# More places in the weight ring until the first projection ends: six, then five, then four again

## What is computed

```
mod = SiLU(cond) @ w_mod[l] + b_mod[l]            # 1024 x 6144, for two vectors cond
h   = RMSNorm(x) * (1 + scale1) + shift1
qkv = h @ w_in[l]                                 # three head groups: A, B and C
x   = x + gate1 * (attention(qkv) @ w_out[l])
h2  = RMSNorm(x) * (1 + scale2) + shift2
x   = x + gate2 * PEER(h2)                        # top 16 of 128^2 experts, 8 heads
```

## Time and profile before

| | us |
|---|---|
| median of 3 runs | 4315.52 (4315.12, 4315.52, 4328.44) |
| the profiled execution, own time | 4312.1 |
| its span | 4310.0 |
| PE busy in the span | 2889.9 |
| DVE busy | 2803.9 |
| ACT busy | 1465.4 |
| POOL busy | 1282.5 |
| mean granted TensorE clock | 0.818 of full |

### The profile page before, as it was taken

The page is one execution under the profiler, slowest core; times in us unless marked ns, Lnnn a source line. Parts: engine busy times, 40 slices in busy tenths (PEclk is TensorE's granted clock), DMA queues, the critical chain, the costliest instruction groups (busy, mean ns, idle before and its releaser), DMA issues.

```text
span 4310.0 us, 47615 instructions
## 1 busy us (share of the span) xinstructions
PE 2889.9 (67%) x16592; PEld 1297.9 (30%) x16592; DVE 2803.9 (65%) x5874; ACT 1465.4 (34%) x4706; POOL 1282.5 (30%) x1306
## 2 busy tenths in 40 slices
PE   6887788766666566665656978886555565555665
PEld 4555565332221122221112566542111111111111
DVE  1167887697646755665675789669764674674554
ACT  2113675322223322222233468533222222222222
POOL 1002222123333333333333222112333333343332
PEclk9898899887887777777877989998777768777767
DMA  8447897669999999999998778666999999999997
GB/s 292 176 154 293 346 361 262 229 248 396 402 414 405 402 411 402 411 408 417 416 408 340 266 252 292 223 228 243 406 419 421 417 415 417 414 416 418 415 421 326
DMA packets 230192, 1508.71 MB, mean 350 GB/s; under 512 B 25408, under 2 KB 29504, under 8 KB 64960
## 3 DMA queue, kind: packets, MB, share of 16 engines
q0 software_dynamic: 185504, 1353.53, 78.4%
q1 hardware_dynamic: 44448, 152.14, 9.6%
HBM read 1501.38 MB, written 4.19 MB: 349 GB/s over the span
## 4 chain that ended last, share of the span: by engine, by line
DMA 41%; PE 26%; DVE 20%; issue 6%; ACT 5%; POOL 2%; SPq 0%; ACTq 0%; DVEq 0%; POOLq 0%
DMA work<-expert_dram,work 39%; PE psum L893 10%; DVE work L1792 5%; PE psum L925 4%; DVE work L1836 3%; PE psum L738 3%; PE psum L831 3%; DVE work L1844 2%; POOL work L2054 2%; ACT work L1266 1%; PE psum L808 1%; DMA ring<-w_mod_dram 1%; PE psum L742 1%; PE psum L792 1%; DVE stat L1580 1%
## 5 line engine op out<-in xcount | busy, mean ns | idle before, releaser
L893 PE MATMUL psum<-work 64*64 64x512 f32 x8192 | 1428.2, 827 | 1103.1 <-ACT work L1266 1103.1
L1792 DVE SCALAR_TENSOR_TENSOR work<-work,psum 128x1024 f32<-128x1024 f32 x1024 | 1247.6, 1220 | 991.2 <-DMA work<-expert_dram,work 987.2
L2054 POOL DMA_INDIRECT work<-expert_dram,work x1024 | 978.4, 955 | 1739.6 <-PE psum L893 1608.1
L893 PEld LDWEIGHTS psum<-work 64*64 64x64 f32 x8192 | 328.8, 168 | 2144.3 <-ACT work L1266 1877.9
L1257 ACT ACTIVATE work<-work 128x2 f32<-128x2 f32 x512 | 104.1, 203 | 1913.4 <-DVE work L1792 1913.3
L2036 POOL DMA_INDIRECT work<-expert_dram,work x256 | 274.7, 1073 | 1180.2 <-DVE work L1836 874.4
L1844 DVE SCALAR_TENSOR_TENSOR work<-work 128x1024 f32<-128x1024 f32 x256 | 313.2, 1224 | 106.0 <-DMA work<-expert_dram,work 105.5
L1266 ACT ACTIVATE work<-const,work 128x128 f32<-128x128 f32 x1024 | 347.4, 386 | 0.0
L1836 DVE SCALAR_TENSOR_TENSOR work<-work 128x1024 f32<-128x1024 f32 x254 | 326.9, 1287 | 15.2 <-ACT work L1297 14.7
L845 PE MATMUL psum<-work,ring 128*128 128x512 f32 x512 | 231.5, 607 | 30.5 <-ACT work L1110 30.5
L1260 ACT ACTIVATE work<-work 128x1 f32<-128x1 f32 x1024 | 245.7, 287 | 16.8
(11 more groups left out here) (199 smaller groups left out, 2887.6 us busy)
## 6 DMA issues: line engine op xcount, KB each, us to landing
ring<-w_mod_dram SPq DMA_DIRECT2D x96, 512.0 KB, 6.1
ring<-w_in_dram SPq DMA_DIRECT2D x80, 512.0 KB, 4.6
ring<-w_query_dram SPq DMA_DIRECT2D x64, 512.0 KB, 6.0
work<-expert_dram,work POOLq DMA_INDIRECT x1280, 8.8
ring<-w_out_dram SPq DMA_DIRECT2D x32, 512.0 KB, 6.5
work<-rpb_dram POOLq DMA_DIRECT2D x2, 2688.0 KB, 17.0
xT<-xT_dram SPq DMA_DIRECT2D x1, 2560.0 KB, 11.8
work<-tables_dram POOLq DMA_DIRECT2D x2, 1024.0 KB, 9.5
```

The source lines that it names most:

```text
L893: last = pe.matmul(out[to:to + HP, cols_], diag[tok, n % NDIAG, tok], rows[(SLOTS * t + s) % NBUF][tok, D + 512 * half:D + 512 * half + 51 ...
L1792: dve.scalar_tensor_tensor(u, u, 1.0, pair[0], ALU.mult, ALU.mult, accum_out=act_in[:, s:s + 1]).then_inc(dot_done, 1)
L2054: pool.indirect_dma_start(rows[m % NBUF], None, a[f"expert{l}"], bass.IndirectOffsetOnAxis(expert[:, t % 2, s:s + 1], 0)).then_inc(row_in[ ...
```

## The change

Two places are added to the ring, in pieces of `work` that are idle for the time: place 4 at `H_AT + KC * NLAT`, place 5 (`SUM_PLACE`) on `csum`. Both serve up to block `win 0 12`; up to `win 0 19` place 4 does; from then on the four of `ring` alone. A block no longer goes to place n % 4 but to the allowed place that was, by a table made at build time, released first: `last[p]` is the number of the block that stood there, and for a `win` of the first layer that number plus `INNER[i]`, the count of blocks that PE takes before it is done with it. The order of the loads, the order of PE's work and all sizes stay. DVE gets one wait more, for all uses of place 5 to be over, ahead of the first write to `csum`.

```diff
+MORE = 2
+SUM_PLACE = RING + 1
+SUM_BLOCK = 13
...
+    place, count, uses, last = [], [], [0] * (RING + MORE), [-1] * (RING + MORE)
+    for n, (what, l, i) in enumerate(ORDER):
+        allowed = RING
+        if n < BLOCK["win", 0, SUM_BLOCK]:
+            allowed = RING + 2
+        elif n <= BLOCK["win", 0, NWIN - 1]:
+            allowed = RING + 1
+        p = min(range(allowed), key=lambda x: last[x])
+        place.append(p)
+        count.append(uses[p])
+        uses[p] += 1
+        last[p] = n + INNER[i] + 0.5 if what == "win" and l == 0 else n
...
+        ring_more = [at(H_AT + KC * NLAT, KC, P), at(X_AT + D, KC, P)]
...
-                if n >= RING:
-                    sp.wait_ge(freed[n % RING], n // RING)
-                sp.dma_start(ring[:, n % RING], weights[what][l, i]).then_inc(landed[n % RING], 16)
+                if COUNT[n]:
+                    sp.wait_ge(freed[PLACE[n]], COUNT[n])
+                sp.dma_start(ring_at(n), weights[what][l, i]).then_inc(landed[PLACE[n]], 16)
...
-                pe.wait_ge(landed[n % RING], 16 * (n // RING + 1))
-                return ring[:, n % RING]
+                pe.wait_ge(landed[PLACE[n]], 16 * (COUNT[n] + 1))
+                return ring_at(n)
...
                     dve.wait_ge(ctx_coef, SLOTS * l + s + 1)
+                    if l == 0 and s == 0:
+                        dve.wait_ge(freed[SUM_PLACE], PLACE.count(SUM_PLACE))
```

More of the change, by code:

```diff
@@ L323, with inner_blocks, ring_places @@
 ORDER = list(BLOCK)
+MORE = 2
+SUM_PLACE = RING + 1
+SUM_BLOCK = 13
+def inner_blocks():
+    out, step = [], 0
+    for parts in FRONT_SEQ:
+        n = 0
+        for p, seq in enumerate(parts):
+            for x in seq:
+                blocks = 1 if x != "f" else FRONT_BLOCKS[step] if step < FRONT else 0
+                step += x == "f"
+                n += blocks if p < len(parts) - 1 else 0
+        out.append(n)
+    return out
+INNER = inner_blocks()
+def ring_places():
+    place, count, uses, last = [], [], [0] * (RING + MORE), [-1] * (RING + MORE)
[10 more added lines that the diff above has]
+        last[p] = n + INNER[i] + 0.5 if what == "win" and l == 0 else n
+    return place, count
+PLACE, COUNT = ring_places()
 def ctx_uses():
@@ L566, in build @@
         ctx_chosen = sem("ctx_chosen")
-        landed = [sem(f"landed{i}") for i in range(RING)]
-        freed = [sem(f"freed{i}") for i in range(RING)]
+        landed = [sem(f"landed{i}") for i in range(RING + MORE)]
+        freed = [sem(f"freed{i}") for i in range(RING + MORE)]
         row_in = [sem(f"row_in{i}") for i in range(NBUF)]
@@ L586, in cblocks, with ring_at @@
             return cbank(*key).rearrange("p (c t) -> p c t", t=P)
+        ring_more = [at(H_AT + KC * NLAT, KC, P), at(X_AT + D, KC, P)]
+        def ring_at(n):
+            return ring[:, PLACE[n]] if PLACE[n] < RING else ring_more[PLACE[n] - RING]
         def exps(l, kind):
@@ L591, in done @@
         def done(*key):
-            return freed[BLOCK[key] % RING], BLOCK[key] // RING + 1
+            return freed[PLACE[BLOCK[key]]], COUNT[BLOCK[key]] + 1
         PROJ = NWIN + HC
@@ L658, in take @@
                 n = BLOCK[key]
-                pe.wait_ge(landed[n % RING], 16 * (n // RING + 1))
-                return ring[:, n % RING]
+                pe.wait_ge(landed[PLACE[n]], 16 * (COUNT[n] + 1))
+                return ring_at(n)
             def release(last, *key):
-                last.then_inc(freed[BLOCK[key] % RING], 1)
+                last.then_inc(freed[PLACE[BLOCK[key]]], 1)
             def mod_tile(l, j):
```

## The result

The changed kernel took 4268.18 us in the median of four runs (4264.52 to 4273.19), against 4315.32 us of the kernel before; the ratio is 0.9889, with a 95% interval of 0.9867 to 0.9912. The forecast was 4279, with a range from 4271 to 4294: the direction and the cause were right, the time fell 2.8 us under the range. Two more series of executions of the same kernel, further down, gave ratios of 0.9910 (0.9893 to 0.9928) and 0.9923 (0.9910 to 0.9937). Over all its 15 executions the changed kernel's median is 4273.0, over 96 executions of the kernel before it is 4311.5: 38.4 us, where 36.5 were forecast.

A forecast was written before the change was run, and what follows sets the result against it. PE was taken to wait in the front for loads stuck behind held `win` blocks, then run at half clock. Savings of 4 + 22.8 + 12.7 - 3 = 36.5 us from 4312.1, plus 3.4 for the median, gave 4279, range 4271 to 4294.

The forecast's parts named there:

- What bounds the front: Up to 270 us, PE waits 25.1 us for ring loads because SP's queue stands behind seven held `win` blocks.
- The opening: Before the first `win` block, six places save 4 us of load waits and transfer time; bounds 0 to 5.5.
- The held blocks: From 45 to 270 us, PE's waits for ring loads go: 22.8 us saved, bounds 18 to 25.1.
- the context's chain: In the context's attention, faster PE work no longer covers DVE and ACT: 3 us lost again, bounds 0 to 6.
- The clock: Five half-speed stretches of PE after long ring waits return to 2.4 GHz: 12.7 us saved, bounds 0 to 13.7.
- The second rival: In the front, the load stalls go but PE's slow clock stays, only elsewhere: 4289 us, chance 17%.
- The sum: Over the front, savings of 4, 22.8 and 12.7 us less 3 lost give 36.5 us.
- the median of the runs is 3.4 higher: For the whole kernel, the runs' median lies 3.4 us above the profiled execution, turning 4275.6 into 4279.
- faster by more than 13 us: For the whole kernel, a gain above the 0.3% taken as measurable was given 95%, within it 3%, slower 2%.
- absorbed: In the front, the context's chain swallows the gain, block 98 moving 10 us or less: 4306 to 4315, chance 5%.
- The rival with POOL's loads: From 44 to 57 us, POOL's table and bias loads delay blocks 22 to 24: 4286, up to 4293, chance 12%.
- Slower: At `csum`, DVE's wait for place 5 becomes real and stalls its queue and PE: for instance 4325, chance 2%.

## Why the forecast was right, and where it was not

*What bounds the front.* Right. SP standing behind a held block was the main cost: the rule alone, on four places, took the seven long waits and 23 to 25 us. That the short waits are loads given too little time is shown by the same kernel against the changed one, 8.6 us with 8.2 of waits. What the prediction did not say is that a count of six in plain turn covers most of it too, with SP standing 87.8 us.

*The opening, 4 us.* The three profiles of each kernel give means of 45.3 and 41.8 for its end, 3.4 us (5.2 in the first pair); against the kernel with only the opening undone it is 2.5 to 4.5. The working was too cautious about the rate and right by the scatter: the stretch now moves 410 GB/s with the DMA share at 1.03, where I had taken 372 from a row.

*The held blocks, 22.8, less 3 for the context's chain.* In the first pair of profiles, 25.1 us of ring waits went; 2.5 came back at L1092 and 2.3 in the chain (2.9 less the 0.6 of before). Net 20.3, forecast 19.8.

*The clock, 12.7.* The time between the first matmul and the first gather fell by 34.1; less the 20.3, 13.8 remain. For the second pair, with 26.7 us of ring waits before, it is 33.2 less 22.1, so 11.1, and for the third, with 24.9, it is 31.6 less 20.4, so 11.2. This is a remainder, not a measurement by itself, but it goes with the slow time, which fell by 29.5, 24.8 and 23.4 us: half of these is 14.8, 12.4 and 11.7. In the kernel with the rule on four places the same sum leaves about 13 us (25.0 less 11.8), beside 14.0 for half of its slow time's fall. The size was right. That it is a cost of its own beside the stalls is not borne out: with the waits kept and the clock held up nothing of it shows in the time. The second rival, stalls gone and clock slow, did not come: in every kernel whose long ring waits went, the slow time fell to 14.3 to 16.0 us by itself. The Trainium skill (TensorE: Matmul & The Clock Gate, "HAM oscillation — how this bites in real kernels") puts the penalty at the throttled time times (1 - 1.2/2.4), an estimate of 15.1 for the 30.2 us of the earlier trace rows. The remainder of 11.1 to 13.8 is under it, and the run with the waits filled, where 13.0 us less of slow time brought nothing, shows a case that such an estimate does not cover: loads that are late.

*The sum.* 36.5 for the front. The means of the first gather over three profiles each are 335.1 and 298.7: 36.4 us. That it comes within 0.1 is luck, since the first gather of one kernel moves by 3 us; that it comes within a few us is not, as the opening (3.4 against 4) and the time between (33.0 against 32.5) do so each.

*The step that failed* is the one from the front's gain to the time of the runs: "From the first gather to the end the time must stay the same within 3 us", the added "the median of the runs is 3.4 higher", and with them a range made of the bounds of the terms alone, with nothing in it for how far executions of one kernel lie apart. The 10.8 us between the forecast and the result are made up so. The front of the first pair gave 39.4 instead of 36.5, 2.9 us (1.2 in the opening, 0.5 in the waits, 1.1 in the remainder). The rest was 3.1 us shorter, just over what the prediction had allowed. And the median, 3.4 us above the profiled execution before, was 1.5 us below it now (4268.18 against 4269.68), which is 4.9 more. The last two are scatter as far as the runs can tell: the executions of one kernel lie up to 30 us apart (4297.91 to 4328.44 before, 4264.52 to 4282.82 after), and in one series of 23 alone 4303.71 to 4326.41; the 4315.5 on which I based the forecast is 4.0 over the median of all executions of that kernel, and the result of 4268.2 is 4.9 under that of its own. What makes the executions differ stays open.

*Slips in the working.* The 95% for "faster by more than 13 us" holds only if part of *absorbed* is counted in, and its 4306 to 4315 lie within 13 us of 4315.5; by the rivals' own numbers it is 91%, and 7% within. The 6.69 us of the 32 matmuls reach 0.7 us beyond the slow stretch that ends at 69.4, so they are not all at half clock, and the saving by their ratio (11.6, not 11.7) is too small; half, 13.7, was the better of the two. Block 20 is issued at 58.6, which is 20.8 us behind the first of the four loads: the 21.11 run to the end of its issue. None of these moves the forecast by more than 1 us.

*The rival with POOL's loads* did not come. Its loads and the ring's ran together from 39 us on. Window of the changed kernel:

```profile
39.00:52.00 13.00, 11.39 (x53) 4.97 (x54) 7.46 (x12) 7.01 (x10) 1.70 (x4) 0.77 1.03 425
```

425 GB/s against 363 in the earlier trace rows; POOL waited 14.5 us for the bias instead of 13.2, for which no other engine waited in turn, and behind 41 us PE waited for no load of the ring. *Absorbed* did not come, since the context's norm and chain took 4.8 us back and not 25. *Slower* did not come: DVE's wait for place 5 appears in no list of waits.

## What to carry to other kernels

When one queue issues loads in order into places taken in turn, look for a buffer that is used across many others: everything behind its next turn stands, and giving each load the place that is free first costs no memory. Here it was worth 24 us of the front, the two further places 8.6 on top; the places alone, taken in turn, were worth 27.5. A slow clock after a stall does not have to be a second cost: with the clock held up while the loads stayed late nothing was gained here, so before you add it to the stall, find out what is late next. And before a range is stated in a few us, it needs the scatter of the executions themselves, which the medians of three runs don't show.

## What had not been expected of the hardware

A wait alone does not say whether the clock falls. Before, two waits around 188 us were followed by the slow stretch from 188.9 to 192.3 of the earlier trace rows; the timeline of PE there:

```profile
187.62 0.61 PE L674 MATMUL psum<-ring,cT 128*2 128x256 f32 x8 [1.88 <-DMA ring<-w_mod_dram]
188.88 5.46 PE L925 MATMUL psum<-work,ring 128*128 128x128 f32 x32 [0.65 <-DMA ring<-w_out_dram]
```

In the kernel with the rule on four places a similar pair, 0.9 us shorter in the first, left it at full speed; its timeline:

```profile
173.67 0.61 PE L715 MATMUL psum<-ring,cT 128*2 128x256 f32 x8 [0.99 <-DMA ring<-w_mod_dram]
174.95 3.84 PE L966 MATMUL psum<-work,ring 128*128 128x128 f32 x32 [0.67 <-DMA ring<-w_out_dram]
```

The same 32 matmuls on the context last 3.84 us here and 5.46 there. Why the one pair lets the clock fall and the other does not is not shown. And 96 executions of one program, each on one core, with identical instructions, lie between 4297.91 and 4328.44 us, over twice the 0.3% (13 us) that the forecast took as the limit of a measurement; the median of the first four is 4315.3, those of six groups of 11 to 23 lie between 4308.0 and 4313.5. The series were not all on the same chip, and what part of this is the chip's is not separated.
